# Layer-norm and latent sums folded before their matmuls, index weights taken from the index key's tile, and one latent tile moved ahead of the key products, in a two-block attention kernel

## The reference, cut to what matters

```python
# first block, for all 2048 tokens
h = x @ w_in                      # split into x_q, x_kv, k_rope_raw, gate_a, u_pool, gate_b
y_a = mla_branch(x_q, x_kv, k_rope_raw, ...) * silu(gate_a)   # rms_norm(x_q) @ w_uq, rms_norm(x_kv) @ w_ukv
y_b = pool_branch(u_pool, ...) * silu(gate_b)
x = layer_norm(alpha * x + concat(y_a, y_b) @ w_out, ln_g, ln_b)

# second block, the same tokens behind 16 meta tokens
proj = h @ w_in_2                 # q_a, c_kv, q_idx, k_idx, w_idx, gate_a, q_h, f_h, i_h, gate_h
s_idx = sum over 4 heads of w_idx * relu(q_idx . k_idx)       # w_idx: 4 numbers per token
a = attention over the top 256 keys by s_idx, on the 128-wide latent rms_norm(c_kv)
r = hgrn2(q_h, f_h, i_h)          # chunked linear recurrence
h = layer_norm(alpha * h + concat(a, r) @ w_out_2, ln_g_2, ln_b_2)

# layer_norm: mean over features, then mean of squares of (x - mean); rms_norm: mean of squares
```

## Time and profile before

| | |
|---|---|
| Median of three runs | 4267.09 us |
| Profiled execution | 4259.95 us, span 4258.2 us |
| Mean granted TensorE clock | 0.953 of full speed |
| TensorE busy | 3913.5 us, 92% |
| VectorE busy | 1794.8 us, 42% |
| ScalarE busy | 1476.0 us, 35% |
| GpSimd busy | 265.0 us, 6% |

### The profile page before, as it was taken

One profiled execution on the slowest core, in us unless ns is written; L12 is line 12 of the kernel. 1 busy time (PEld: TensorE's weight loads), 2 busy tenths in 40 slices (PEclk: granted clock), 3 DMA queues, 4 the chain that ended last, 5 costly groups with the idle time before them and its releaser, 6 DMA issues.

```text
span 4258.2 us, 41374 instructions
## 1 busy us (share of the span) xinstructions
PE 3913.5 (92%) x15538; PEld 2252.0 (53%) x15538; DVE 1794.8 (42%) x4182; ACT 1476.0 (35%) x2458; POOL 265.0 (6%) x328
## 2 busy tenths in 40 slices
PE   7899999999999999999889898899789998788996
PEld 3345644654565456455554445644457744346772
DVE  3313222312222132136532676417785417776631
ACT  1213311322231223123321554305664405774441
POOL 0001001000100010011100111001010001010000
PEclk8999999999999999999889998999889999898998
DMA  4120023002201200322021110111100111110011
GB/s 152 53 91 19 1 69 104 1 20 79 75 1 45 79 30 1 107 74 72 20 75 55 62 55 1 60 57 64 45 20 1 60 59 55 38 35 1 1 39 41
DMA packets 70919, 204.16 MB, mean 48 GB/s; under 512 B 6296, under 2 KB 7872, under 8 KB 70464
## 3 DMA queue, kind: packets, MB, share of 16 engines
q1 hardware_dynamic: 61344, 183.67, 12.9%
q10 hardware_dynamic: 9376, 17.84, 1.1%
HBM read 184.69 MB, written 16.79 MB: 47 GB/s over the span
## 4 chain that ended last, share of the span: by engine, by line
PE 80%; ACT 8%; DVE 7%; issue 3%; DMA 1%; SPq 0%; POOL 0%; ACTq 0%; DVEq 0%; POOLq 0%
PE bank L1589 35%; PE o_acc L1943 6%; PE o_acc L1716 6%; PE bank L1684 5%; PE bank L1911 4%; PE bank L1688 3%; ACT ql L914 3%; PE bank L1807 2%; PE bank L1709 2%; PE bank L1935 2%; PE bank L1597 2%; PE bank L1636 2%; PE bank L1841 2%; ACT prob_t L1044 2%; PE bank L1915 1%
## 5 line engine op out<-in xcount | busy, mean ns | idle before, releaser
L1589 PE MATMUL bank<-group_even,weights 128*128 128x512 f32 x1376 | 607.1, 600 | 16.0 <-DMA weights<-in_w_in_kv 11.5
L1589 PE MATMUL bank<-group_odd,weights 128*128 128x512 f32 x1376 | 603.0, 596 | 5.9 <-ACT tmp L900 5.9
L1589 PE MATMUL bank<-y_all,weights 128*128 128x512 f32 x1024 | 447.7, 599 | 11.8 <-DMA weights<-in_w_out 5.3
L1589 PEld LDWEIGHTS bank<-group_even,weights 128*128 128x128 f32 x1376 | 263.0, 193 | 340.2 <-issue 340.2
L1589 PEld LDWEIGHTS bank<-group_odd,weights 128*128 128x128 f32 x1376 | 261.2, 192 | 329.0 <-issue 328.8
L1170 DVE CUSTOM_DVE_ANT_0 probs<-bank,mask 128x512 f32<-128x512 f32 x256 | 161.5, 687 | 417.8 <-PE bank L1688 417.8
L1589 PEld LDWEIGHTS bank<-y_all,weights 128*128 128x128 f32 x1024 | 196.3, 192 | 258.6 <-issue 258.6
L1943 PE MATMUL o_acc<-v,prob_t 128*128 128x64 f32 x2176 | 290.3, 282 | 45.5 <-ACT prob_t L1044 45.5
L1943 PEld LDWEIGHTS o_acc<-v,prob_t 128*128 128x128 f32 x2176 | 269.6, 197 | 77.9 <-ACT prob_t L1044 77.9
L1044 ACT ACTIVATE prob_t<-bank 128x512 f32<-128x512 f32 (+3 forms) x320 | 160.2, 531 | 392.0 <-PE bank L1935 392.0
L854 ACT ACTIVATE prob_t<-bank 128x512 f32<-128x512 f32 x256 | 145.9, 596 | 430.2 <-PE bank L1709 430.2
(11 more groups left out here) (343 smaller groups left out, 4881.5 us busy)
## 6 DMA issues: line engine op xcount, KB each, us to landing
weights<-in_w_in SPq DMA_DIRECT2D x101, 512.0 KB, 3.5
weights<-in_w_in_q SPq DMA_DIRECT2D x64, 512.0 KB, 3.5
weights<-in_w_out SPq DMA_DIRECT2D x64, 512.0 KB, 3.5
weights<-in_w_i SPq DMA_DIRECT2D x20, 512.0 KB, 3.6
group_even<-in_x_t SPq DMA_DIRECT2D x8, 1024.0 KB, 7.9
group_odd<-in_x_t SPq DMA_DIRECT2D x8, 1024.0 KB, 9.1
group_even<-x_t SPq DMA_DIRECT2D x8, 1024.0 KB, 8.3
group_odd<-x_t SPq DMA_DIRECT2D x8, 1024.0 KB, 7.2
```

Source lines behind the costliest of these rows:

```text
L1589: ins = M(bank(*name)[:], ring[n % SLOTS][:, k * P:(k + 1) * P], rhs[:, k, :], start=(k == 0), stop=(k == chunks - 1))
```

## The change

It has three parts.

1. **Sums.** GpSimd adds the 8 residual slices of a group into `probs[:, 0:TB]` with seven additions, each behind the residual of its slice, and the mean is then one matmul (2 instructions) on the total. The variance's 8 squares are added by VectorE in three additions of 2048, 1024 and 512 columns, and then one matmul; only the last variance of the kernel keeps its 8. GpSimd adds the 4 query squares with three additions, and `q_sq` is one matmul.
2. **Index weights.** The `ki` chunk's second 64 columns, before a copy of the key, now hold the 4 index-weight columns 16 times over. VectorE makes two copies of the key half and a third of the weights' half into `o_sb`; TensorE transposes four 64x128 blocks. `f` 0 moves ahead of the variance. The constant `w_wi` and its load go.
3. **Order of the latents.** `kv` 0 of group g+1 is put between `kv_sq` of group g and the wait for `k_normed`; `lat` is used in two halves.

```diff
 def first_pair_steps(g):
-    yield from [("kv", g, j) for j in range(2)]
+    if g == 0:
+        yield ("kv", g, 0)
+    yield ("kv", g, 1)
     yield ("krope", g)
     yield ("kv_sq", g)
+    if g + 1 < G:
+        yield ("kv", g + 1, 0)
...
-    yield from [("ki", g), *norm["2mean"], ("qi", g, 0), ("qi", g, 1), *norm["2square"], ("wi", g), *norm["2var"], ("f", g, 0), *first[0],
+    yield from [("ki", g), *norm["2mean"], ("qi", g, 0), ("qi", g, 1), *norm["2square"], ("wi", g), ("f", g, 0), *norm["2var"], *first[0],
...
+        def sum_squares(tag, g, dve, V, sq):
+            dve.wait_ge(squared, KC * (g + 1 + (0 if tag == "1" else G)))
+            for w in (4, 2, 1):
+                ins = V.tensor_tensor(sq[:, 0:w, :], sq[:, 0:w, :], sq[:, w:2 * w, :], ALU.add)
+                if w > 1:
+                    sum_square(dve, ins)
+            ins.then_inc(ln_summed, 1)
...
         @block.gpsimd
...
+            def sum_features(tag, g):
+                total, x_t = probs[:, 0:TB], x_of(g)
+                wait_drained(pool, tag + "out", g, 0)
+                for c in range(1, KC):
+                    wait_drained(pool, tag + "out", g, c)
+                    ins = pool.tensor_tensor(total, x_t[:, 0, :] if c == 1 else total, x_t[:, c, :], ALU.add)
+                    if c < KC - 1:
+                        sum_of(pool, ins)
+                ins.then_inc(ln_summed, 1)
+            def sum_query_squares(g):
+                for j in range(1, 4):
+                    pool.wait_ge(q_sq_made, 4 * g + j + 1)
+                    ins = pool.tensor_tensor(y_of(g)[:, 0, :], y_of(g)[:, 0, :], y_of(g)[:, j, :], ALU.add)
+                    if j < 3:
+                        sum_of(pool, ins)
+                ins.then_inc(q_summed, 1)
...
             for g in range(G):
+                if g > 0:
+                    sum_features("1", g - 1)
+                sum_query_squares(g)
...
+            sum_features("1", G - 1)
             second_begins(pool)
             for g in range(G):
+                if g > 0:
+                    sum_features("2", g - 1)
...
+            sum_features("2", G - 1)
...
         @block.scalar
...
-                latents("kv", g, 2, prob_t, VEC["kv_g"], ("v", g - 1, BG - 1) if g else None)
+                kv_latents(g, range(0 if g == 0 else 1, 2))
                 root(("kv_sq", g), KVR, 0, (k_normed, g) if g else None)
+                if g + 1 < G:
+                    kv_latents(g + 1, range(1))
...
         @block.vector
...
                 V.tensor_tensor(lat[:], lat[:], wide(rstd[:], 4), ALU.mult).then_inc(q_normed, 1)
                 if g > 0:
+                    sum_squares("1", g - 1, dve, V, sq_view(probs))
                     normalise("1", g - 1, dve, step, V)
...
             centre("1", G - 1, dve, V)
+            sum_squares("1", G - 1, dve, V, y_all)
...
                     if kind == "2mean":
                         centre("2", st[1], dve, V)
+                    elif kind == "2square":
+                        sum_squares("2", st[1], dve, V, y_of(g))
...
                     elif kind == "ki":
                         wait_tile(dve, *st)
-                        drains(V.tensor_copy(ki[:, g * TB:(g + 1) * TB], bank(*st)[:]), *st)
+                        for e in range(2):
+                            step(dve, V.tensor_copy(ki[e * DH2:(e + 1) * DH2, g * TB:(g + 1) * TB], bank(*st)[0:DH2, :]))
+                        drains(V.tensor_copy(o_sb[DH2:P, :], bank(*st)[DH2:P, :]), *st)
...
         @block.tensor
...
                 squares(("kv_sq", g), prob_t, 2)
+                if g + 1 < G:
+                    wait_x(pe, g + 1, (g + 1) // 2)
+                    project(("kv", g + 1, 0), x_of(g + 1), KC)
                 pe.wait_ge(k_normed, g + 1)
...
             def mean_of(tag, g):
-                for c in range(KC):
-                    wait_drained(pe, tag + "out", g, c)
-                squares((tag + "mean", g), x_of(g), KC)
+                pe.wait_ge(ln_summed, ln_sums(tag, g, 0))
+                squares((tag + "mean", g), probs[:, 0:TB].unsqueeze(1), 1)
             def variance_of(tag, g, sq):
+                if (tag, g) != ("2", G - 1):
+                    pe.wait_ge(ln_summed, ln_sums(tag, g, 1))
+                    squares((tag + "var", g), sq, 1)
+                    return
...
-                for j in range(4):
-                    wait_drained(pe, "xq", g, j)
-                squares(("q_sq", g), y_of(g), 4)
+                pe.wait_ge(q_summed, g + 1)
+                squares(("q_sq", g), y_of(g), 1)
...
                     elif kind == "wi":
+                        wait_drained(pe, "ki", g)
                         claim(*st)
                         for b in range(BG):
-                            for k in range(KC):
-                                ins = M(bank(*st)[:, b * HI:(b + 1) * HI], x_of(g)[:, k, b * P:(b + 1) * P], w_wi[:, k, :],
-                                        start=(k == 0), stop=(k == KC - 1))
+                            ins = nc.tensor.transpose(bank(*st)[:, b * DH2:(b + 1) * DH2], o_sb[DH2:P, b * P:(b + 1) * P],
+                                                      ident[DH2:P, DH2:P])
```

More of the change, by code:

```diff
@@ L431, in program @@
         brk = alloc(two, "brk", [P, 5, BG])
-        w_wi = alloc(two, "w_wi", [P, KC, HI])
         mx = alloc(two, "mx", [P, H2, 8])
@@ L547, in program @@
         gates_made = sem("gates_made")
+        sum_step = sem("sum_step")
+        square_step = sem("square_step")
+        ln_summed = sem("ln_summed")
+        q_sq_made = sem("q_sq_made")
+        q_summed = sem("q_summed")
         stored2 = sem("stored2")
@@ L1114, in _ @@
                 step(dve, V.reciprocal(rstd[:], std[:]))
[L1115 removed]
+                kv_lat = lat[:, 2 * (g % 2):2 * (g % 2) + 2, :]
+                V.tensor_tensor(kv_lat, kv_lat, wide(rstd[:], 2), ALU.mult).then_inc(k_normed, 1)
                 for h in range(H1):
@@ L1601, in _ @@
             for g in range(G):
-                wait_x(pe, g, g // 2)
-                for j in range(2):
-                    project(("kv", g, j), x_of(g), KC)
+                if g == 0:
+                    wait_x(pe, g, 0)
+                    project(("kv", g, 0), x_of(g), KC)
+                project(("kv", g, 1), x_of(g), KC)
                 project(("krope", g), x_of(g), KC)
@@ L2013, in lay_out @@
     w2 = np.asarray(inp["w_in_2"])[0]
-    cols2 = [c0 + ar(P), ki0 + np.tile(ar(DH2), 2)] + [qi0 + j * P + ar(P) for j in range(2)]
+    cols2 = [c0 + ar(P), np.concatenate([ki0 + ar(DH2), wi0 + np.tile(ar(HI), DH2 // HI)])] + [qi0 + j * P + ar(P) for j in range(2)]
     for start in (q0, ga0, hq0, hf0, gh0):
```

35 lines of the change are left out of this document (21 added, 14 removed).

## The result

Four runs of the changed kernel gave 4125.44 to 4135.50 us, median 4132.43; four of the kernel before, on the same chip, a median of 4264.04. The ratio of the two is 0.9689, with a 95% interval of 0.9669 to 0.9708: 131.6 us less. That is inside the forecast range and 11 us above the forecast time of 4121. The profiled execution took 4125.44 us, the fastest of the four, with a span of 4123.6, at the same mean clock as before, 0.953.

What follows compares the result with a forecast made beforehand. The prediction took TensorE, busy for 92% of the span, to bound the kernel. Its six terms summed to 145.9 us saved, which off the median of 4267.09 us gave 4121 us, with a range of 4101 to 4146 us.

Steps and rivals of the forecast that it cites:

- The bound: Whole kernel: TensorE, busy 92% of the span, bounds it; removing its instructions pays unless the stage waits for another engine.
- Keys and values: First block, keys: next group's latent tile fills TensorE's idle time before the key products, 0.5 us wait left; 26.2 us saved.
- Query projections: First block: `q_sq` saves 2.6 us four times, means 6.0 three times, variances nothing after wait and clock loss; 28.4 us.
- Between the blocks: Mean and variance between the blocks: 7.2 us saved (4 to 10), with a 4.8 us wait and 2.6 us clock loss.
- Index weights, group 0: Four transposes replace 64 small matmuls: 8.5 us plus 3.0 of clock loss behind them, 11.5 us saved.
- Second block: Groups 1 to 3: first index read 22.5 us earlier each, VectorE's sum in time by 2.5 us; 67.5 us saved.
- The rival in which the rounds of the bisection absorb it: Second block: ScalarE and VectorE rounds absorb the 67.5 us; only 78 us saved, 4189 us; chance 6%.
- the one in which the edit does not do it: Tile and sums leave TensorE waiting as before; only index weights and end count, 51 us saved, 4216 us; chance 3%.
- The end: Last mean: one GpSimd addition and one matmul replace 16 instructions, 5.1 us saved; the last variance stays.
- Contention: GpSimd's 68 new additions could slow VectorE through SBUF access; priced at nothing, at most 6 us.
- The slower rival: Waits of 4.2 us at three first-block variances drop the clock far into the attention behind, making the kernel slower; chance 2%.
- The rival of a better clock: Added waits cost no clock and fewer low stretches follow later, so more is saved: 4104 us; chance 14%.

Runs made afterwards that it cites:

- The later variants: Changed kernel with first-block variance one tile later (4104.86 us); also a query tile in the last key wait (4098.62); also two first-attention waits filled (4094.91).

## Why the prediction was right

**The bound.** That an instruction off TensorE is worth its place in the queue, unless the stage waits for another engine, held: the sum of the touched stages is 146.3 us, forecast 145.9. That the two are so close is in part luck: single stages were missed by up to 2.2 us, in both directions, and these misses cancel.

**Keys and values** (26.2): the wait that is left, the period (36.9 for 36.6) and group 3's unchanged wait came as forecast; undoing it costs 25.1 in its stage.

**Query projections** (28.4): `q_sq` and the means as forecast. The variances were the step with the least certain price, a saving of 6.0 against a wait of 4.2 and a clock loss of 1.8. The wait measured 3.9, the loss at the tile behind it 1.8 and at the matmul itself 1.0, and undoing them moves nothing (386.8, 385.1, 385.1 against 385.8, 385.7, 385.7). So each variance lost 0.7 us more than forecast, 2.1 in all. Against it stand two stretches of 3.4 us at the low clock, at 922 and 1318 in the kernel before, which the changed one has not: 1.7 us each. Together that is the 1.3 us by which the stage beats the forecast. So the total is near because two misses offset each other. The second trace of the kernel before has two such stretches too, at 530 and 1318, and none of the three traces of the changed kernel has one; why is open.

**Between the blocks** (7.2, measured 9.4) the forecast wait of 4.8 us ahead of the variance did not come. Timeline of TensorE after:

```profile
1720.19 1.92 PE L1662 MATMUL bank<-probs,ones 128*128 128x512 f32 x2
1721.90 13.67 PE L1816 MATMUL bank<-x_meta,weights 128*128 128x16 f32 x64
1736.02 2.08 PE L1662 MATMUL bank<-y_all,ones 128*128 128x512 f32 x2 [0.45 <-DVE y_all L616]
1738.03 8.04 PE L1834 MATMUL bank<-weights,x_meta 128*16 128x512 f32 x16
```

The small meta products, which I had at 9.1 us, take 13.7 at the low clock. In the kernel before, the 16 instructions of the mean ran among them and the clock was up again at 1778.8; now the mean has two and the clock stays down from 1716.2 to 1740.1. The variance comes no later for it, since it waits for the chain through VectorE: from the mean to the end of the variance it is 17.9 us, forecast 17.7. So up to there 9.4 us are saved of 9.8. The term that was mis-sized is the loss behind it, 2.6 us: the next tile takes 8.04 where it took 7.04, 1.0 more, and most of that is given back by faster small matmuls behind it, so that, counted from the last first-block scores, the meta scores start 9.2 us earlier.

**Index weights, group 0** (11.5, measured 10.3): the low clock reaches the meta scores at the start of this stage. Timelines of TensorE, before and then after:

```profile
1816.55 5.26 PE L1780 MATMUL bank<-index,qa 128*128 128x512 f32 x8
```

```profile
1751.45 6.51 PE L1851 MATMUL bank<-index,qa 128*128 128x512 f32 x8
```

These 1.25 us are what is missing, and belong to the 2.6 us that were forecast one stage earlier.

**Second block** (67.5, measured 67.7): the full cover of the sum of squares, priced at 2.5 us to spare, is seen in the rows of group 1. The rival in which the rounds of the bisection absorb it is out: the stretches from the index rows to the attention grow by 0.6, 0.9 and 1.1 us in groups 1 to 3, not by the 22.5 saved. So is the one in which the edit does not do it.

**The end** (5.1, measured 2.9) was a little mis-sized. GpSimd's addition takes 1.26 us, and I had priced it at 1.04, from a GpSimd subtraction in which one of the two operands repeats single columns; the last addition ends 1.4 us behind the last residual, where 1.1 was the sign to look for. From the end of the last residual to the reading of the mean it is 2.6 us, 7.4 before: 4.8 saved. The other 1.9 us are not of the change. Most of them, 1.7 us, go in the output projection ahead of the last residual, in a low stretch that the kernel before does not have there. Window of the changed kernel, with the clock at 0.50:

```profile
4023.60:4027.00 3.40, 3.40 (x6) 1.32 (x5) 0.00 (x0) 0.00 (x0) 0.00 (x0) 0.50 0.02 5
```

The two repeats of the changed kernel lack this stretch, and the stage takes 101.4 and 99.7 us in them, 3.8 and 5.4 less than before.

**Contention** was priced at nothing, at most 6. It is seen in three places, one in each of the groups 1 to 3 of the first block, 2.8 us of VectorE in all. VectorE, group 1 of the first block, beside the last addition of GpSimd, which runs from 555.77 to 557.15:

```profile
556.06 1.37 DVE L1135 TENSOR_SCALAR tmp<-tmp 128x512 f32<-128x512 f32 x1
557.47 0.43 DVE L1136 TENSOR_SCALAR tmp<-tmp 128x512 f32<-128x512 f32 x1
```

0.9 us more for the same operation; it ends 0.3 us behind GpSimd's. TensorE does not wait for it there. The Trainium skill (SBUF — State Buffer, Who interferes with whom) calls the pair of ports that both use an exclusive lock. The trace fits that in one point, that VectorE's instruction ends only behind GpSimd's; which ports they used it does not show. No residual runs beside an addition of GpSimd in any trace, so no run here shows what one costs there; the sum had it at nothing.

**The clock** is what is missing between the touched stages and the time: 131.6 us came of 145.9, and the time is 11 us above the forecast. In the profiled pair 8.1 us of it are in the attention stage of group 0 and 3.6 in the other stages not touched. The forecast put the effect of the change on these stages at nothing in its sum, and had 9 us for them in its range, from the spread of the three runs. That allowance and the slack of the other terms kept the time inside the range, not the sum. Whether the loss comes from the change is open, as said above. The profile that I worked from had the shorter of the two measured stages, 109.1 us, and was below all three runs beside it, 7 us under their median, which is why the forecast was taken off the median. The slower rival is out: the low stretch behind each variance is 6.8 us long and ends well before the scores. The rival of a better clock, 4104 us, did not come either. The later variants, at 4095 to 4105 us, show its mechanism in part; they also take away the waits themselves, which that rival had kept.

## What to carry to other kernels

Price an instruction that leaves the bounding engine by the stage it stands in, and before folding a sum onto another engine ask what that engine has in its queue: here moving the matmul one tile later was worth 20 us, and folding it without that nothing. Compare kernels by stages between common landmarks as well as by medians, when a stage that nobody touched can vary by 9 us in one and the same program; take two or three profiles of each kernel to see which stages do. And where the stages add up to more than the medians give, as here by 14 us or more, do not put the rest down to noise. Where TensorE waits a few us ahead of a long run of small matmuls, try to fill the wait with the next tile, or with work that is thrown away.

## What was not expected of the hardware

- The low clock can last long while TensorE works. In the attention stage of group 0, the longest low stretch was 30.7 and 61.4 us in two traces of the kernel before, 61.4, 81.9 and 81.9 in three of the changed one, and 105.8 in the version with the old order. Between the best and the worst of these the stage grew from 109.1 to 136.0 us, with 44.6 and 109.6 us of low clock in the whole stage: 0.4 us for each. What decides how long it lasts in one run is open.
- With ten instructions of 512 columns in each of two waits of about 5 us the longest low stretch was 17.1 us in two kernels, and in one of them the four times lay within 3.1 us.
- A GpSimd addition of two full 512-column float32 operands takes 1.26 us, 1.38 beside a VectorE instruction, against 1.04 for the subtraction with repeated columns in the earlier trace rows.
